# Expert matmuls of the middle experts written out, and one late weight unit sent unevenly

## The reference, cut to what matters

```python
hb = swiglu_clamped(u[tok] @ w1[e] + b1[e])      # w1[e]: 1024 x 2048
yb = (hb @ w2[e] + b2[e]) * wt[:, None]          # w2[e]: 1024 x 1024
acc.at[tok].add(yb)
```

## Time and profile before

| | us |
|---|---|
| median of 3 runs | 1379.71 |
| the profiled execution | 1376.83 |
| its span | 1375.0 |
| PE busy | 1310.6 (95%) |
| DVE busy | 380.6 (28%) |
| ACT busy | 282.7 (21%) |
| HBM read | 466.61 MB |
| instruction fetches (q8) | 71 packets, 1.16 MB |

### The profile page before, as it was taken

How to read it: one execution, slowest core, us unless ns; L and a number is a source line. 1 busy time by engine, 2 the same in 40 slices (tenths; PEclk the granted TensorE clock), 3 DMA queues, 4 the chain that set the end, 5 groups by cost and what they waited for, 6 DMA issues and landing times.

```text
span 1375.0 us, 18199 instructions
## 1 busy us (share of the span) xinstructions
PE 1310.6 (95%) x7380; PEld 662.1 (48%) x7380; DVE 380.6 (28%) x949; ACT 282.7 (21%) x638; POOL 24.2 (2%) x40
## 2 busy tenths in 40 slices
PE   9999999999999999998999999989999999998996
PEld 6677787557885433433343333333333333333332
DVE  2256466675121611211121112111112111112112
ACT  3136334473001211111111111111111111111111
POOL 4000000000000000000000000000000000000000
PEclk9999999999999999999999999999999999999999
DMA  8842443445947799999999999999999999999995
GB/s 291 264 127 91 153 153 122 112 134 181 313 164 306 293 412 429 438 426 429 431 432 429 432 427 431 434 428 427 436 430 428 432 431 429 432 429 432 430 425 209
DMA packets 62399, 469.28 MB, mean 341 GB/s; under 512 B 3589, under 2 KB 36633, under 8 KB 48076
## 3 DMA queue, kind: packets, MB, share of 16 engines
q1 hardware_dynamic: 58780, 457.63, 81.5%
q0 software_dynamic: 1952, 5.61, 1.4%
q10 hardware_dynamic: 1584, 4.78, 1.0%
HBM read 466.61 MB, written 1.13 MB: 340 GB/s over the span
## 4 chain that ended last, share of the span: by engine, by line
PE 65%; DMA 30%; DVE 3%; issue 1%; ACT 1%; POOL 0%; SPq 0%; DVEq 0%
PE bank L1373 62%; DMA ring<-in_w 15%; DMA arena<-in_w 15%; PE bank L1839 1%; PE bank L1787 1%; DVE arena L1275 0%; DVE arena L1277 0%; DVE arena L1274 0%; DVE arena L1273 0%; PE bank L1495 0%; ACT arena L658 0%; PE bank L1682 0%; PE bank L1497 0%; DVE arena L1003 0%; DVE ring L1039 0%
## 5 line engine op out<-in xcount | busy, mean ns | idle before, releaser
L1373 PE MATMUL bank<-ring,arena 128*64 128x512 f32 (+1 forms) x2024 | 502.6, 606 | 23.1 <-DMA ring<-in_w 22.4
L1373 PE MATMUL bank<-arena 128*128 128x64 bf16 (+6 forms) x3162 | 402.5, 382 | 25.0 <-issue 11.2
L1373 PEld LDWEIGHTS bank<-ring,arena 128*64 128x64 f32 (+1 forms) x2024 | 175.4, 144 | 305.7 <-issue 296.9
L1373 PEld LDWEIGHTS bank<-arena 128*128 128x128 bf16 (+3 forms) x3162 | 176.6, 122 | 254.0 <-issue 233.9
L1373 PE MATMUL bank<-arena,ring 128*128 128x256 f32 (+4 forms) x1408 | 283.3, 379 | 1.6 <-ACT ring L680 1.5
L1373 PEld LDWEIGHTS bank<-arena,ring 128*128 128x128 f32 (+1 forms) x1408 | 229.8, 180 | 47.2 <-issue 4.8
L1273 DVE TENSOR_SCALAR arena<-bank 128x256 f32<-128x256 f32 x64 | 27.1, 423 | 721.3 <-PE bank L1373 721.3
L853 ACT ACTIVATE arena<-arena 128x256 f32<-128x256 f32 x64 | 26.7, 417 | 517.6 <-DVE arena L1273 517.6
L1373 PE MATMUL bank<-arena,wdt 64*128 64x512 f32 (+1 forms) x280 | 66.7, 603 | 1.7 <-issue 1.7
L862 ACT ACTIVATE arena<-bank 128x512 f32<-128x512 f32 x32 | 19.1, 597 | 215.0 <-PE bank L1373 215.0
L1373 PEld LDWEIGHTS bank<-arena,wdt 64*128 64x128 f32 (+1 forms) x280 | 23.2, 181 | 44.5 <-issue 41.8
(11 more groups left out here) (255 smaller groups left out, 576.6 us busy)
## 6 DMA issues: line engine op xcount, KB each, us to landing
ring<-in_w SPq DMA_DIRECT2D x48, 4096.0 KB, 40.6
arena<-in_w SPq DMA_DIRECT2D x34, 4096.0 KB, 40.2
ring<-in_w SPq DMA_DIRECT2D x18, 2048.0 KB, 14.8
ring<-in_w_in SPq DMA_DIRECT2D x34, 1024.0 KB, 6.9
arena<-in_w SPq DMA_DIRECT2D x9, 2048.0 KB, 10.0
ring<-in_w_ssm SPq DMA_DIRECT2D x8, 1024.0 KB, 8.7
ring<-in_w_att SPq DMA_DIRECT2D x16, 256.0 KB, 7.2
ring<-in_w_out SPq DMA_DIRECT2D x4, 1024.0 KB, 4.9
```

The costliest lines, as they stand in the source:

```text
L1373: return tn.matmul(o, lhsT, rhs, start=first, stop=last, skip_group_check=True)
```

## The change

Two edits. On PE the loop over experts 2 to 26 is replaced by the same instructions written out 25 times. On SP, unit 85 (expert 28, the second half of its w1, place 0) is sent in another way: its first 5120 words of every row in one transfer of 128 rows, then the last 3072 words (three eighths) of rows 0 to 125 in 21 transfers of six rows each, row r, r+21, ..., r+105, and those of rows 126 and 127 in one more. These 22 share a new semaphore `uneven_loaded`, for which PE waits beside the old one before it reads the unit.

```diff
-        LAST_UNITS = UNITS - 4
+        LAST_UNITS, UNEVEN_UNIT, FIRST_ENGINES, EVEN_WORDS = UNITS - 4, 85, 6, 10 * (2 * BUF // 16)
...
+            def uneven_unit(u, used):
+
+                sp.wait_ge(slot_used, used)
+                dst, src = places[u % PLACES], unit_source(u)
+                sp.dma_start(dst[:, 0:EVEN_WORDS], src[:, 0:EVEN_WORDS]).then_inc(place_loaded[u % PLACES], 16)
+                each = P // FIRST_ENGINES
+                rest = each * FIRST_ENGINES
+                for r in range(each):
+                    sp.dma_start(dst[r:rest:each, EVEN_WORDS:], src[r:rest:each, EVEN_WORDS:]).then_inc(uneven_loaded, 16)
+                if rest < P:
+                    sp.dma_start(dst[rest:P, EVEN_WORDS:], src[rest:P, EVEN_WORDS:]).then_inc(uneven_loaded, 16)
...
             for u in range(2 * PLACES + rounds * ROUND, LAST_UNITS):
-                unit(u, u // 3, free_at(u))
+                if u == UNEVEN_UNIT:
+                    uneven_unit(u, free_at(u))
+                else:
+                    unit(u, u // 3, free_at(u))
...
                 pe.wait_ge(place_loaded[u % PLACES], rounds * 16 * 3 + 16 * (u // PLACES) + 16)
+                if u == UNEVEN_UNIT:
+                    pe.wait_ge(uneven_loaded, 16 * (P // FIRST_ENGINES + (P % FIRST_ENGINES > 0)))
...
-            rounds = (E - 4) // PLACES
-            with pe.Fori(0, rounds) as i:
-                for e in range(2, 2 + PLACES):
-                    expert(i * PLACES + e, 0, 3 * e, lambda u: unit_arrived(u, i))
-            for e in range(2 + PLACES * rounds, E - 2):
+            for e in range(2, E - 2):
                 expert(e, 0, 3 * e, unit_arrived)
```

More of the change, by code:

```diff
@@ L273, in hybrid_layer @@
                              "esig_ready", "hs_ready", "hT_ready", "hT_saved"))
-        b_ready, gw_ready, ye_saved, last_sc_ready, fin_ready, fin_by_act, hg_ready = (sem(n) for n in (
-            "b_ready", "gw_ready", "ye_saved", "last_sc_ready", "fin_ready", "fin_by_act", "hg_ready"))
+        b_ready, gw_ready, uneven_loaded, ye_saved, last_sc_ready, fin_ready, fin_by_act, hg_ready = (sem(n) for n in (
+            "b_ready", "gw_ready", "uneven_loaded", "ye_saved", "last_sc_ready", "fin_ready", "fin_by_act", "hg_ready"))
         def cols_of(w, c0, kt=KT, k0=0, n=256):
```

## The result

The changed kernel takes 1397.03 us (median of four runs, 1396.42 to 1397.56) against 1379.62: a ratio of 1.0128 with a 95% interval of 1.0116 to 1.0140, 17.4 us slower. The profiled execution took 1397.56 us with a span of 1395.5; that of before lay 2.8 us under its median, so the two spans differ by 20.5 us, and that is what the trace has to explain.

The account below looks back on a forecast made before the run. Bound by DMA transfers, by the slowest of 16 engines: the last landing goes from 10.5 to 15.8 us behind the first, +5.3 us, the loop's 2.0 us gain vanishing, giving 1385.0 us, range 1376.4 to 1391.

Parts of the forecast that it names:

- the late eight: DMA engines at the end: 8 of 16 stand 10 us behind, put there by uneven instruction fetches.
- The 1.6 us a fetch: DMA engines, 469 to 1350: each of 50 instruction fetches costs one engine 1.6 us (8 x 10 us / 50).
- Part 1's 2.0 us vanishes, since the late group isn't last any more: Written-out expert loop: its 2.0 us gain on the late engines doesn't count, as the six senders land last.
- 22 transfers more at 0.33 us: SP at unit 85: about 0.38 us each with gaps, 8.4 us, hidden by the queue.
- The row of the 64-partition loads: Profile row: 192 GB/s against 366 to 128 partitions, same DMA share; read as each eight-partition group having its own way.
- The senders' own term: Unit 85's six senders: the worst takes 19.1 us for its 21 pieces, 25.2 against 9.7, falling back 15.5 us.
- Only the six engines' own ways are free: Unit 85's pieces: 0.46 us on a free way, 0.92 us on one shared by two.
- 15.5 and 0.3: Last landing 15.8 us behind the first: 15.5 us a sender falls back, 0.3 estimated spread among the early eight.
- rival (b): Some of unit 85's six senders are fetch-laden late engines: with shared ways 24 us behind, +13.5 (1393); chance 0.12.
- The signs for part 1: Written-out loop: about 40 fetches from 469 to 1350, not 50, and no 2.5 us "issue" gap on PE.
- Rival (a): Ways into partitions don't bind, an engine is the limit: 0.8 to 3.8 us gained, likeliest 2.9, 1376.8; chance 0.28.
- rival (c): Unit 85's uneven part is neutral: pieces meet ways free half the time, 0.69 us each; -2 to +1, 1379; chance 0.15.

Follow-up runs that it names:

- the twins: Changed kernel with eight six-row transfers for 22, rest of unit 85's last three eighths unsent: rows 4 apart 1374.94 us, rows 21 apart 1381.46 us.

## Why the prediction was wrong

It said 1385.0 (1376.4 to 1391.0), slower with 0.58; it is 1397.0. The direction held, the size didn't, by a factor of 3.

**What bounds the kernel, and the late eight.** Right: the landings set the end, and the 50 fetches put eight engines back. The 1.6 us a fetch held. A fetch packet takes 1.07 us and the 32 KB packet right behind it about 1.7 instead of 1.22, together 1.55 us lost, in each of the 43 fetches of the kernel before that the trace lets pair with their packet; and 10 fetches fewer brought 2.3 us on the last engine in the kernel with the loop alone written out, where 2.0 was forecast, bounds 1.6 to 3.2. Wrong was the step "Part 1's 2.0 us vanishes, since the late group isn't last any more": the last to land is a late engine, and the written-out loop is worth 5.1 us beside the uneven unit.

**SP and the queue.** The step "22 transfers more at 0.33 us" was mis-sized: a six-row transfer takes SP 0.66 us. This is the row after:

```profile
L490 SPq DMA_DIRECT2D arena<-in_w x21: 660/661/827, 1220.7 to 1234.9; - x21
```

With the gaps that is 0.70 us for each, and unit 86 was issued at 1236.1, 15.8 us after unit 85 and not 8.4. It stayed hidden all the same: the first engine finishes unit 85's even part at 1248.9, and the DMA share is 1.00 through the dent.

**The ways in.** The row of the 64-partition loads was read rightly: a group has its own way in, moving the sender doesn't move the target, a shared way halves. The senders' own term came out too: 19.1 us for the pieces of the worst sender, and the five early engines needed 19.0 on average. The step that failed is what this costs everybody else. The forecast let a piece slow only the way that it shares ("Only the six engines' own ways are free") and put the senders 15.8 us behind a first engine that lost nothing. Measured, with more than one intruder all sixteen halve, 222 GB/s for 19.5 us; the first engine, spared 3.6 us of unit 85, still lands 7.8 us later. These 7.8 us stand in no case of mine. The five early senders are among the twelve engines that land 15.1 to 18.9 us behind where the first one landed before, about as forecast, but they are no more the worst.

**The late engine.** The other step that failed is that all six senders stand among the early eight (the 0.3 in "15.5 and 0.3"): one of the six doesn't. That was rival (b), which I gave 0.12: with shared ways it forecast 24 us behind the first and +13.5. Measured 22.9 and +12.2; with the 7.8 us it gives the 20.0 of the landings. The rival was right in its mechanism. That its size fits so well is in part luck: the late engine stood only 6.0 us behind the first, not 8.3 (the kernel with rows 4 apart shows it undisturbed, 1254.6 for 1248.5), the half pace made that 11.4, its pieces took 20.5 us and not 19.1, and the first engine's own loss takes part of this out of the difference. I had noted that the trace doesn't name the engines, and then held six of six early to be far likelier than it was: eight of sixteen are late, and nothing in the trace said which.

In the terms of the sum: forecast were 0 for the first engine and 5.3 us more between first and last; measured were 7.8 and 12.2.

**The rest.** PE's wait ahead of unit 85 was forecast at 6 us and is 16.57. The long tail of a few engines was forecast at a share near 0.2 for 8 us and is 0.11 for 12; the sign of rival (b), a tail of over 20 us, is there. The signs for part 1 held: 39 fetches from 469 to 1350, no "issue" gap. Rival (a), that ways don't bind, is refuted by the twins; rival (c) also, whose pieces take 0.69 us where nearly all took 0.81 to 0.97. One slip changes nothing in the sum: by the bits that the prediction names, row 63 lies in the lower half, in the eighth group, which isn't one of the six engines' either.

The Trainium skill (DMA: Bandwidth & Descriptors, "Why a DMA increments its semaphore by 16") says that a transfer of six rows runs on the six lowest engines; the runs agree in the number, six streams for six rows, five for five, three for three and two for two; which engines they are, no trace names. It also has a sentence ("Back-pressure in remote DMA") that a saturated port "clogs the path back to the source SDMA engines and to any SDMA engines sharing that AXI path", told of transfers between cores. It would fit sixteen slowed by two; that one alone slows none but its host isn't in it, and no run here shows the path itself. What makes the second intruder different stays open.

## What to carry to other kernels

When transfers run at the full pace of the core, each group of eight partitions is as full as each engine: handing an engine's rows to another one moves no byte out of the full group. In each run here where two or more engines wrote into groups in use, all sixteen went at half pace. A transfer of few rows does no harm in the partitions that its engines would fill anyway (0.46 us a piece); one to other partitions had better wait until the stream is over. And before a sum rests on which engines a transfer uses, it pays to find out which of them are late. What did pay was taking load off the engines themselves: fewer turns of a long loop, fewer instruction fetches beside the stream, 2.55 us for an edit of five lines; the kernel with that edit alone is the fastest of the full ones here (1376.42 us).

## What the runs showed of the hardware

- An instruction fetch of 16 KB costs the engine that carries it 1.55 us beside a full stream (50 of them put eight engines 10 us back), though 16 KB of weights take 0.61. By the landings they fall on eight of the sixteen engines; of six engines that a six-row transfer uses, one is late, and the five of a five-row transfer are not.
- Each turn of the long loop cost on average 2.5 fetches more than written-out code (50 and 40 from 469 to 1350), as well as 2.4 to 2.8 us of PE.
- One engine writing into a busy group slows itself and its host, 430 to 388 or 399 GB/s. Two or more slow all sixteen, to 199 to 231 GB/s, at a DMA share near 1 (0.96 to 1.11).
- A transfer of six rows took SP 0.66 us where one of 128 took 0.33.
